# Sums of the last two tiles' rows moved from VectorE to TensorE banks, behind the experts of a two-block transformer kernel

## The reference, cut to what matters

```python
x = x + hierarchical_moe(...)          # each token: two rows come back from its experts
x = rms_norm(x, norm_final_g)          # end of the first block
...
def short_conv_mixer(x, ln_g, w_in, conv_w, w_out):
    h = rmsnorm(x, ln_g)
    b_gate, c_gate, u, z = jnp.split(h @ w_in, 4, axis=-1)
```

## Time and profile before

| | us |
|---|---|
| median of 3 runs | 1481.57 |
| lowest, highest | 1480.69, 1484.92 |
| the profiled execution, its own time | 1485.3 |
| its span, first to last instruction | 1483.5 |
| TensorE busy in it | 1350.4 |

### The profile page before, as it was taken

How to read it: one execution, slowest core, us unless ns; L and a number is a source line. 1 busy time by engine, 2 the same in 40 slices (tenths; PEclk the granted TensorE clock), 3 DMA queues, 4 the chain that set the end, 5 groups by cost and what they waited for, 6 DMA issues and landing times. The chain is left out here.

```text
span 1483.5 us, 16786 instructions
## 1 busy us (share of the span) xinstructions
PE 1350.4 (91%) x6344; PEld 898.8 (61%) x6344; DVE 537.0 (36%) x1074; ACT 418.9 (28%) x814; POOL 388.9 (26%) x372
## 2 busy tenths in 40 slices
PE   7999998999999899888888888777999999999899
PEld 5777766898768733333223223226888887787567
DVE  3649947430242511111111111127310415564653
ACT  5333365163331100000000000025222224344631
POOL 7553223168320112111111111100445440000321
PEclk9999988999999799999999999988999999999999
DMA  7221221244205879999999999973322322221100
GB/s 210 73 100 57 94 78 66 86 161 142 85 5 213 363 316 420 421 423 420 423 423 421 423 422 422 423 314 126 113 86 93 106 86 85 85 86 57 57 22 36
DMA packets 72368, 298.27 MB, mean 201 GB/s; under 512 B 10168, under 2 KB 10216, under 8 KB 51568
## 3 DMA queue, kind: packets, MB, share of 16 engines
q1 hardware_dynamic: 64848, 282.80, 48.6%
q0 software_dynamic: 7456, 14.59, 3.0%
HBM read 293.16 MB, written 12.58 MB: 206 GB/s over the span
## 5 line engine op out<-in xcount | busy, mean ns | idle before, releaser
L749 POOL TENSOR_TENSOR ring_rounded<-ring,ring_rounded 128x512 fp32r<-128x512 f32 x192 | 251.3, 1345 | 348.2 <-ACT ring_rounded L1467 348.2
L876 PE MATMUL bank<-HT_rounded,ring_rounded 128*128 128x512 f32 (+1 forms) x576 | 221.2, 384 | 3.2 <-DVE ring_rounded L2367 1.9
L878 PE MATMUL bank<-HT_rounded,ring_rounded 128*128 128x512 f32 (+1 forms) x576 | 217.6, 378 | 0.0
L877 PE MATMUL bank<-ring_rounded 128*128 128x512 f32 (+1 forms) x576 | 217.4, 378 | 0.0
L1177 PE MATMUL bank<-ring,B 128*64 128x512 f32 x704 | 176.6, 654 | 37.2 <-DMA ring<-in_w 36.2
L1177 PEld LDWEIGHTS bank<-ring,B 128*64 128x64 f32 x704 | 54.3, 148 | 143.4 <-issue 109.2
L2259 DVE TENSOR_TENSOR B<-bank,small 128x512 f32<-128x512 f32 x32 | 22.1, 691 | 324.5 <-PE bank L1167 324.5
L878 PE MATMUL bank<-ring_rounded 128*128 128x512 f32 x352 | 138.9, 395 | 0.0
L1467 ACT ACTIVATE ring_rounded<-ring 128x2048 fp32r<-128x2048 f32 x54 | 102.7, 1913 | 113.2 <-DMA ring<-in_w_in_a 46.9
L876 PEld LDWEIGHTS bank<-HT_rounded,ring_rounded 128*128 128x128 f32 x576 | 108.4, 188 | 30.1 <-issue 5.9
L877 PEld LDWEIGHTS bank<-ring_rounded 128*128 128x128 f32 x576 | 108.4, 188 | 20.2 <-issue 1.0
(11 more groups left out here) (391 smaller groups left out, 1994.6 us busy)
## 6 DMA issues: line engine op xcount, KB each, us to landing
ring<-in_w SPq DMA_DIRECT2D x88, 1024.0 KB, 30.3
A<-in_w SPq DMA_DIRECT2D x21, 2048.0 KB, 28.6
ring<-in_w SPq DMA_DIRECT2D x11, 2048.0 KB, 28.8
XN<-in_w SPq DMA_DIRECT2D x20, 1024.0 KB, 29.2
HT<-in_w SPq DMA_DIRECT2D x20, 1024.0 KB, 32.3
ring<-in_w_in_a SPq DMA_DIRECT2D x16, 1024.0 KB, 5.1
ring<-in_w_in SPq DMA_DIRECT2D x14, 1024.0 KB, 7.4
ring<-in_w_in_b SPq DMA_DIRECT2D x8, 1024.0 KB, 5.3
```

Source lines behind the costliest of these rows:

```text
L749: last = pool.tensor_tensor(r32(lo), lo, r32_read(quarter(g, True)[:, k, :]), ALU.subtract)
L876: pe.matmul(o, r32(a_hi), r32(b_hi), start=first, stop=False)
L877: pe.matmul(o, r32(a_hi), r32(b_lo), start=False, stop=False)
L878: return pe.matmul(o, r32(a_lo), r32(b_hi), start=False, stop=last)
```

## The change

x of tiles 2 and 3 is put into four banks (two per tile) by a matmul with the identity, and the two rows that come back are added there by further matmuls with the identity: two matmuls of 128x512 f32 for x, four for the rows, per tile. ScalarE squares the sums from the banks (two halves per tile, whose sums VectorE adds), VectorE scales them from the banks into `x3g`. VectorE's `add_back` and `scale_final` of these tiles go, and so do ScalarE's `square_x3(2)` and `(3)`; `add_back` 0 and 1 stay. The four banks are new uses "x3", opened behind x4_t of tiles 0 and 1 (eight banks), so that c 0 to 3 now take the banks of x4_t 0 and 1, and x4_t of tiles 2 and 3 those of x3. On TensorE the order is: x of tiles 2 and 3, wait for x3 of tile 0, seven spins, rows of tile 2, turn 0, rows of tile 3, turn 1, two spins, c0. Tile 2 is still turned behind column 1 of c0's first half, tile 3 behind column 2 instead of column 3; the four `fill`s for both stand ahead of the first column.

```diff
--- before.py
+++ after.py
@@ -197,7 +197,8 @@
 
 def second_plan():
 
-    first = [(("x4_t", t, b), "dve") for t in range(NT) for b in range(2)]
+    rows = lambda name, ts: [((name, t, b), "dve") for t in ts for b in range(2)]
+    first = rows("x4_t", (0, 1)) + rows("x3", (2, 3)) + rows("x4_t", (2, 3))
     plan = [(("c", j), "act") for j in range(4)]
     for half in range(2):
         for name, by in (("c", "act"), ("u", "dve"), ("z", "act"), ("b", "dve")):
@@ -205,7 +206,7 @@
                 plan += [((name, j), by) for j in range(4 * half, 4 * half + 4)]
     by = dict(first + plan)
     closed = [what for what, _ in first + plan]
-    opened = closed[0:4] + [("c", j) for j in range(4)] + closed[4:8] + closed[12:]
+    opened = closed[0:8] + [("c", j) for j in range(4)] + closed[8:12] + closed[16:]
 
     def uses(engine, whats, opens=True, closes=True):
 
@@ -1260,25 +1261,43 @@
 
             done[0] = 0
 
-            def turn_x4(t):
-
-                for b in range(2):
-                    o = fill(V, "x4_t", t, b)
-                    if t == 0 and b == 0:
-                        pe.wait_ge(sem("x3_ready"), 1)
-                        spin(o, 9)
-                    pe.wait_ge(sem("x4n_ready"), t + 1)
+            def turn_x4(t, outs, more=0):
+
+                pe.wait_ge(sem("x4n_ready"), t + 1)
+                for b, o in enumerate(outs):
                     for k in range(4):
                         last = pe.transpose(o[:, P * k:P * k + P], y_back[t][:, 0, 4 * b + k:D:KD], ident)
-                    last.then_inc(bank_filled, 1)
-
-            turn_x4(0)
-            turn_x4(1)
+                    last.then_inc(bank_filled, 1 + more * b)
+
+            first_turned = [[fill(V, "x4_t", t, b) for b in range(2)] for t in range(2)]
+            summed_rows = {t: [fill(V, "x3", t, b) for b in range(2)] for t in (2, 3)}
+
+            def add_row(t, row, first=False, last=False):
+
+                for b, o in enumerate(summed_rows[t]):
+                    ins = pe.matmul(o[:, :], ident, row[:, 512 * b:512 * b + 512], start=first, stop=last)
+                return ins
+
+            def add_rows_back(t):
+
+                pe.wait_ge(sem(f"y_back{t}"), 32)
+                add_row(t, y_back[t][:, 0, :])
+                add_row(t, y_back[t][:, 1, :], last=True).then_inc(sem("x3_summed"), 1)
+
+            for t in (2, 3):
+                add_row(t, x_rows[:, t, :], first=True)
+            pe.wait_ge(sem("x3_ready"), 1)
+            spin(first_turned[0][0], 7)
+            add_rows_back(2)
+            turn_x4(0, first_turned[0])
+            add_rows_back(3)
+            turn_x4(1, first_turned[1], 4)
             outs = [fill(V, "c", j) for j in range(4)]
             part = chunk("c0")
-            spin(outs[0], 4)
+            spin(outs[0], 2)
             for h in range(2):
                 wait_emptied(pe, V["x4_t", 2 * h + 1, 1])
+                turned = [fill(V, "x4_t", t, b) for t in (2, 3) for b in range(2)] if h == 0 else []
                 at = slice(2 * P * h, 2 * P * h + 2 * P)
                 for j, o in enumerate(outs):
                     for k in range(KD):
@@ -1286,8 +1305,8 @@
                                       lambda k: (hT[:, k, at], lowT[:, k, at]), k, k == 0, k == KD - 1)
                     if h == 1:
                         last.then_inc(bank_filled, 1)
-                    elif j % 2 == 1:
-                        turn_x4(2 + j // 2)
+                    elif j in (1, 2):
+                        turn_x4(j + 1, turned[2 * j - 2:2 * j])
             for n in range(2):
                 for name in ("cuzb" if n else "uzb"):
                     to_cols(f"{name}{n}", V, [(name, 4 * n + m) for m in range(4)], hT, lowT)
@@ -1690,6 +1709,16 @@
                 act.wait_ge(sem("x3_ready"), t + 1)
                 sums(x_rows, t, 16 + t)
 
+            def square_x3_summed(t):
+
+                act.wait_ge(sem("x3_summed"), t - 1)
+                for b in range(2):
+                    n = summed[0]
+                    summed[0] += 1
+                    act.wait_ge(sem("ss_ready"), n - 1)
+                    act.activation(E[:, D * (n % 2):D * (n % 2) + 512], bank[V["x3", t, b].bank][:, :], ACT.Square,
+                                   accum_out=ss[:, 16 + t + 48 * b:17 + t + 48 * b]).then_inc(sem("ss_ready"), 1)
+
             def square_x3g(t):
 
                 act.wait_ge(sem("x3g_ready"), t + 1)
@@ -1707,11 +1736,11 @@
             for t in range(2):
                 square_x3g(t)
                 roots(16 + 2 * t, 18 + 2 * t)
+            square_x3_summed(2)
             high_x4(0)
             high_x4(1)
-            square_x3(2)
+            square_x3_summed(3)
             square_x3g(2)
-            square_x3(3)
             roots(20, 22)
             square_x3g(3)
             roots(22, 24)
@@ -2342,10 +2371,25 @@
                 dve.wait_ge(sem("x3_ready"), t + 1)
                 dve.tensor_tensor(x3g[t], x_rows[:, t, :], g_fin, ALU.mult).then_inc(sem("x3g_ready"), 1)
 
+            def scale_summed(t):
+
+                for b in range(2):
+                    o = filled(V["x3", t, b])
+                    at = slice(512 * b, 512 * b + 512)
+                    dve.wait_ge(sem("ss_ready"), summed + (5, 7)[t - 2] + b)
+                    last = dve.tensor_tensor(x3g[t][:, at], o[:, :], g_fin[:, at], ALU.mult)
+                    if b == 0:
+                        last.then_inc(done, 1)
+                own(last)
+                dve.nop().then_inc(done, 1)
+                dve.nop().then_inc(sem("x3g_ready"), 1)
+
             def normalise_x4(t):
 
                 c = 16 + 2 * t
-                dve.wait_ge(sem("ss_ready"), summed + (3, 4, 6, 8)[t])
+                dve.wait_ge(sem("ss_ready"), summed + (3, 4, 9, 10)[t])
+                if t >= 2:
+                    own(dve.tensor_tensor(ss[:, 16 + t:17 + t], ss[:, 16 + t:17 + t], ss[:, 64 + t:65 + t], ALU.add))
                 own(dve.tensor_scalar(ms[:, c:c + 1], ss[:, 16 + t:17 + t], 1.0 / D, EPS, ALU.mult, ALU.add))
                 own(dve.tensor_scalar(ms[:, c + 1:c + 2], ss[:, 20 + t:21 + t], 1.0 / D, None, ALU.mult))
                 dve.scalar_tensor_tensor(ms[:, c + 1:c + 2], ms[:, c:c + 1], EPS, ms[:, c + 1:c + 2], ALU.mult, ALU.add)\
@@ -2371,11 +2415,11 @@
             for h in range(2):
                 low_half("c0", h)
             for step, t in ((add_back, 0), (add_back, 1), (scale_final, 0), (scale_final, 1), (normalise_x4, 0),
-                            (normalise_x4, 1), (add_back, 2), (low_x4, 0), (low_x4, 1), (scale_final, 2),
-                            (add_back, 3), (normalise_x4, 2), (scale_final, 3), (normalise_x4, 3), (low_x4, 2),
+                            (normalise_x4, 1), (low_x4, 0), (low_x4, 1), (scale_summed, 2),
+                            (scale_summed, 3), (normalise_x4, 2), (normalise_x4, 3), (low_x4, 2),
                             (low_x4, 3)):
                 step(t)
-            ss_total[0] += 2 * NT
+            ss_total[0] += 2 * NT + 2
             own(dve.memset(vbuf[:, :, 0:CONV2 - 1], 0.0))
             for h in range(2):
                 low_half("u0", h)
```

## The result

| | before | after |
|---|---|---|
| median of 20 executions each, us | 1481.84 | 1486.2 |
| lowest, highest | 1477.52, 1486.98 | 1480.19, 1495.79 |
| the profiled execution, its own time | 1485.3 | 1484.58 |
| its span | 1483.5 | 1482.8 |

The ratio of after to before is 1.0033 (95%: 1.002 to 1.0046): slower by 4.9 us, 3.0 to 6.8. The two profiled executions don't show this in their spans: that of before lies 3.5 us over its median, that of after 1.6 under it. So I compare stretches, and count time from one mark that both kernels have: the start of the spins that follow x3 of tile 0 (1005.60 before, 1006.66 after). "Second half" is the first matmul of c0's second half, which is where every wait of this place has been paid.

A forecast was written before the change was run, and what follows sets the result against it. TensorE, busy for 91% of the span, was taken as the bound. A chain delay of 3.6 us plus 1.7 us of low clock gave +5.3 on 1481.57: 1486.9 us, range 1481.0 to 1490.5, likeliest case 1485.2 to 1488.6.

The forecast's parts named there:

- What could be won: TensorE behind the experts, 1013.3 to 1036.4 us: some 3.7 us of idle time is all an edit there can win.
- x into the banks, spins: TensorE before the row sums: four matmuls, 3.4 to 6.9 us, hidden in idle time; seven spins for nine; both cost 0.
- Row sums of tile 2, start: TensorE waits for y_back2's second transfer, landing at 1013.3 after 11.5 us; tile 0's turns queue behind, 3.1 us later.
- the rows land early: Rival at y_back2's second landing: by 1010.3 everything moves 3.0 us up, to +0.6, 1482.2; chance 0.18 together with misread order.
- Row sums, size: TensorE's four matmuls per tile, 0.86 us each at full clock, taken from an earlier stage: 3.4 us a tile.
- Turns: TensorE: tile 0's turns start near 1016.7, 3.1 us later than before; tile 1's near 1021.1, 5.3 us later.
- Low parts and gate: Ahead of c0: low parts done at 1023.8, then 2.7 us of VectorE scaling frees banks; c0 starts at 1026.5, 5.9 late.
- Inside c0's first half: TensorE: 13.6 us without waits at either turn, where it was 15.83 with them; a gain of 2.3 us.
- Sum of the chain: c0's second half starts at 1040.1 instead of 1036.45: +3.6 us before any clock effect.
- The clock at c0, +1.7 us: TensorE nearly idle ahead of c0, so the clock halves for 3.3 us under the product: 1.7 us, bounds 0 and 3.4.
- clock stays full: Rival at c0: two spins and staggered waits keep the clock up; +3.6, 1485.2 us, within 0.3%; chance 0.25.
- VectorE's relief would not make c0 earlier: Ahead of c0: 7.3 us come off VectorE, yet c0 starts at 1026.5 instead of 1020.6, 5.9 us late.

The follow-up runs named there:

- e6: e2 with tile 3's row sums moved behind tile 1's turns, into the wait for its low parts; 1482.98 us, 0.999 of before.
- e7: Changed kernel with only tile 3 summed on TensorE, behind tile 1's turns; tile 2 on VectorE, late fills, nine spins, none before c0; 1480.43 us, 0.9982 of before.
- e9: The changed kernel measured once more, unedited, beside e10 on one chip; 1484.92 us, 1.002 of before.
- e1: Changed kernel with the fills of tiles 2 and 3 moved from ahead of c0 to directly before their turns; 1483.1 us, 1.0008 of before.
- e4: Changed kernel with nine spins for seven, and five for two ahead of c0; 1485.06 us, 1.0019 of before.
- e10: Changed kernel with six spins for two ahead of c0; 1484.34 us, 1.0004 of before.
- e12: Changed kernel without the two spins ahead of c0; 1489.1 us, 1.0059 of before.
- e3: Changed kernel with TensorE's order turn 0, row sums of tile 2, turn 1, row sums of tile 3; 1489.62 us, 1.0045 of before.
- e8: Kernel before with one edit: tile 3 turned behind column 2 of c0's first half, not column 3; 1480.13 us, 0.9984 of before.
- e2: As e1, and also without the two spins ahead of c0; 1481.31 us, 0.9996 of before.
- e5: Changed kernel with only the second of the two returned rows added for tiles 2 and 3; 1481.59 us, 0.9995 of before.
- e11: Kernel before with adds of tiles 2 and 3 on GpSimd, tile 3 turned behind column 2, low parts first, two spins for four; 1483.24 us, 0.9996 of before.

## Why the prediction was right, and where its sum was not

It said 1486.9 us and slower; 1486.2 was measured, with c0's start as the place and the waits in the order given. That the number came out so near is partly luck, as its steps show:

- *What could be won:* 3.7 us of idle time was called all that any edit here can win. The four spins ahead of c0, 2.71 us, are in the busy time of that sum though they do no work; the room was 6.4 us, and e6 and e7 take 2.2 and 2.1 of it.
- *x into the banks, spins:* hidden, as said; the spins had ended 0.86 us before the rows landed.
- *Row sums of tile 2, start:* the first mis-sized term. The transfers landed after 9.1 and 10.0 us, as these two rows of after's DMA issues say, not after 10.1 and 11.5:

```profile
A<-y_dram SPq DMA_DIRECT2D x1, 512.0 KB, 9.1
...
A<-y_dram SPq DMA_DIRECT2D x1, 512.0 KB, 10.0
```

  From the spins' start it was 6.1 us (6.6 in e9), where the step had 7.7. That the rows land early was a rival; it holds by half, and each us of it was worth one, as that rival said. Counted from the spins, the landing lies below the rival's 1012.5 (1011.75 in before's time), and yet the ratio, 1.0033, is a little over 0.3%.
- *Row sums, size:* 3.54 us from the start to turn 0 for tile 2, 3.43 for tile 3; the step had 3.44. The row of an early stage was a sound price.
- *Turns:* 9.7 and 14.0 where the step gives 11.1 and 15.5: the landing, nothing else.
- *ScalarE:* two squares out of a bank, 0.60 + 0.19 us each, in 1.2 us instead of 1.4, hidden:

```profile
1016.55 0.60 ACT L1719 ACTIVATE E<-bank 128x512 f32<-128x512 f32 x1 [1.63 <-PE bank L1278]
1017.71 1.08 ACT L1731 ACTIVATE HT_rounded<-bank 128x512 fp32r<-128x512 f32 x2
```

- *Low parts and gate:* from turn 1 to c0 5.6 us (the step 5.4); the scaling took 3.1 of it instead of 2.7. e1 takes the gate away and c0 starts 2 us nearer to turn 1, so it is a cost of the place where the `fill`s stand, not of the sums.
- *Inside c0's first half:* 13.35 us with no wait; the step had 13.6.
- *Sum of the chain:* +2.15 us in after's profile and +2.65 in e9's, where the step had +3.6. The difference is the early landing, 1.6 and 1.1, less small terms. With the landings of e4 and e10, whose added spins are hidden, it is +3.2 and +3.0, so the chain of this kernel costs 2.2 to 3.2 us.
- *The clock at c0, +1.7 us:* **the step that failed** in every profile of after. The granted clock is 1.00 there in both, which the prediction itself had named as a sign of being wrong. e12 shows the mechanism and its price, 2.1 us. The rival "clock stays full" had the reason that fits these two profiles, but two spins are no guarantee: e3 had them too, and its clock fell at c0. The Trainium skill ("TensorE: Matmul & The Clock Gate", Part 1) has the clock follow how busy TensorE has lately been; e3 and e12 agree (0.50 behind waits of 3.06 and 4.59 us), and what I had wrong was to count on the fall: with two spins the clock may fall or hold.

So the landing was put too late, the clock term is not seen where it was put, and the sum was still near: the chain shows 2.2 to 3.2 us of the measured 4.9. **What stays open** is the rest, 1.7 to 2.7 us. Part of it may be nothing: the interval begins at 3.0 us, and measured again (e9) the same kernel gave 1.002, which is its position. Part of it goes with the granted clock somewhere in the execution: within the four series of before (105 executions) the time rises by 0.29 us for each us at half clock (correlation 0.80), in after's own twenty by 0.29 (0.87). After's mean clock, 0.9672, is higher than before's in those series (0.9653 to 0.9664), but that doesn't rule the clock out. Around this place, where TensorE often waits or spins and a low clock costs little, before spends more time at half clock than after. The same stretch of before and of after:

```profile
985.00:1040.00 55.00, 35.01 (x205) 28.20 (x204) 36.77 (x48) 28.28 (x41) 1.96 (x2) 0.81 0.43 154
```

```profile
985.00:1040.00 55.00, 38.28 (x201) 26.48 (x196) 30.71 (x47) 26.26 (x43) 1.96 (x2) 0.91 0.43 157
```

That is 21 us at half clock against 10; the stretch has 0.81 in e8's profile too, and 0.91 in e9's and e10's. If other executions are like these, after's twenty have about 8 us more than before's at half clock in all other places (97 less 10, against 100 less 21), and at 0.29 that is some 2 us, the size of the rest. This is an estimate from a few profiles, and whether the change brings it about is open. That some executions of after lose the clock at c0, as e12 and e3 do, was seen in no profile of it. The series of spins, 0, 2 and 6 with ratios 1.0059, 1.0033 and 1.002, and 1.0004, and the missing long executions of e4 and e10 speak for it; e9's profile, a long one with full clock at c0, speaks against it as the whole cause.

The forecast that VectorE's relief would not make c0 earlier was right, but not for want of a place: before, the two adds of tile 2 (2.4 us) stood between the normalised rows and the low parts, on the way to c0, and without them e2 takes 3.0 us from turn 1 to c0 where before took 4.8 (0.9 of the difference is the clock at turn 1). In after the wait for the banks took this back (5.6 us), and the sums came ahead of both turns in TensorE's queue. e5 to e7 turn this round. e6 keeps every sum on TensorE and only moves tile 3's behind turn 1 and the banks' wait behind c0's start, without the two spins: the second half goes from 33.0 to 28.7 us.

## What to carry to other kernels

Work moved to the engine that bounds a kernel is free only where that engine waits anyway: put it behind what is ready sooner and is waited for, and look for the exact gap (here the wait for the low parts, about 3 us, took in four matmuls of 0.86 and left c0 with next to no wait). Ask for a resource (a bank, a buffer) at its first use, not where a list of them is convenient to write; the early `fill`s held a ready product back by about 2 us. And try the smallest part of a change by itself: turning the tiles a column sooner gave, alone, half of what the best rebuilt versions gave by position (1.0 of 2.2 us), and a time that can't be told from the best of theirs.

## What the runs showed of the hardware that was not expected

- **GpSimd and VectorE hinder each other.** In e11 VectorE's 128x1024 operations beside GpSimd's adds took 3.01 us (1.29 alone) and 2.38 (1.22 alone), and a 128x1 operation 1.94 where its like takes 0.16; GpSimd's adds took between 2.34 and 3.35. The Trainium skill ("SBUF — State Buffer", "SBUF: two separate sides") says that a VectorE operation with two SBUF inputs and a GpSimd operation that reads SBUF lock each other out for a whole instruction. The times agree: VectorE's 128x1 operation of 1009.89 ends at 1011.83, where GpSimd's add ends (1011.81); the operation of 1012.30 ends 1.1 us behind GpSimd's second add (1014.23); and GpSimd's third add, begun at 1014.19 while that operation still runs, takes 3.35 us. VectorE's operations with one input in SBUF kept their time beside the same adds:

```profile
1009.70 0.15 DVE L2356 TENSOR_SCALAR small<-small 128x1 f32<-128x1 f32 x1
1015.24 1.27 DVE L2373 TENSOR_TENSOR ring_rounded<-bank,HT_rounded 128x512 fp32r<-128x512 f32 x2
```

- **A few spins between two waits bear on the clock, but two don't settle it.** With two between the waits ahead of c0 it stayed full in both profiles of after and fell in e3's; with none it fell in e12's, and c0's first two columns took 2.1 us more. With five or six, which cost nothing, no execution of 23 took over 1486.8 us (14 of 32 with two).
- **The clock spreads the times.** The twenty executions of before differ by 9.5 us, and the time rises by about 0.29 us with each us at half clock (105 executions of before, correlation 0.80); one profiled execution therefore can't show an effect of 0.3% in its span, only in the stretch where it arises.
